# RWKV scan on one core: the last level of the chunk inverse is applied to the solution, one square and one sum share their weights, and half of the turned blocks are made by transposes

## The chip, the cores and the metric

The kernel runs on one core of one Trainium2 chip. The metric is the device time of one execution, in microseconds (us). The kernel computes a two-layer block and a final mixture of experts; the change touches one stage of it, the scan of the second layer's RWKV mixer.

## The reference

Only the scan matters here. For each of 16 heads of width 64, and for two directions (forward over the tokens, and reversed), a 64x64 state is carried over 256 context tokens and then 512 latent tokens:

```python
def step(s, inp):
    rt, wt, kt, vt, at, bt = inp
    sa = jnp.einsum('bhij,bhj->bhi', s, at)
    s = s * wt[:, :, None, :] + sa[..., None] * bt[:, :, None, :] + vt[..., None] * kt[:, :, None, :]
    y = jnp.einsum('bhij,bhj->bhi', s, rt) if with_out else None
    return s, y
```

The output y is wanted for the latent tokens only. All is float32.

## The kernel before, in words

**Chunks.** The scan goes by chunks of 64 tokens. Inside a chunk the rule "each token's correction depends on those of the tokens before it" is a triangular system of 64 unknowns, so a chunk needs the inverse X of a triangular 64x64 matrix. The inverse does not depend on the state and is made ahead. Then the state streams through the chunks: a right-hand side `rh` from state and values, the solution `uu` = X times the right-hand side, then the output `out` and the next state `zz`.

**Units.** A unit n (0 to 23) is one pair of heads (m = n // 3) and one third of the tokens (256), in both directions. It has 4 chunks per direction, and two heads side by side on the partitions 0 to 63 and 64 to 127 (`halves`). Every small product is therefore 64 rows by 64 columns, and is issued twice, once for each head: `blocks` multiplies four chunks, `turned` transposes blocks by a product with the identity, `gram` makes the products of the operands. One `yield` stands behind each pair of such products. Groups called crossed put a head's result on the other head's partitions, straight ones leave it where it is, so a crossed pair and a straight pair use the four quarters of the array between them.

**The inverse.** `gram` gives P and the masked 16-wide diagonal blocks N (`NP` holds N and its transpose). X = I + N, then three squarings (`squares 0` to `squares 2`) with three sums (`X add` 0 to 2) invert the 16-wide blocks. Two levels follow (16 to 32, 32 to 64). Each makes P·X (`PX`), masks it (`M`), and adds a product with the turned X (`X turned`, copied to `XT`): `XM` 1 and `XM` 2. Between them `XMT` brings the turned X up to date as well.

**The stream.** In each unit and chunk position `sub` (0 to 3): PE `rh` (L2585, L2591), ACT copies it (L2955), PE `uu` (L2605), ACT copies it (L2960), PE `out` (L2621, L2625, L2629) and `zz` (L2647, L2650, L2654), DVE scales the new state (L2845), and the next `rh` needs that.

**Order.** The order of the work on each engine is written down in tables (`CROSSED_AT`, `STRAIGHT_AT`, `WHOLE_AT`, `ACT_AT`, `DVE_AT`, `POOL_AT`). A step of unit n stands at 12n + its number; each engine issues its steps in the order of these numbers and waits only for semaphores. On PE, `together` merges three sorted lists (crossed, straight, whole-array products), a pair of products taking 0.06 on this scale. PSUM has 8 banks, taken in turn, and a product's bank is taken when its group is issued.

**Lines.** L2557 is `blocks` (both squares, sums, PX, XM, XMT), L2567 is `turned` (X turned, bk, v turned), L2548 is `gram` (gram, ka, br). L2823, L2829, L2833, L2835 and L2839 are DVE's sums and masks of the inverse, L2983 is ACT's copy of squares 0 and 1, L2987 of squares 2, L2992 of the turned X.

Of the kernel before, what the change touches and what calls it, by code (L numbers as in the profile page):

```python
# [548 lines left out]
def plan_layer1(K, w_at):  # L549
# [28 lines left out]
    r.NP = K.flat(1024).rearrange("p (d x g c) -> p d x g c", d=2, x=2, g=4)  # L578
    r.Pf, r.Arb = ([K.alloc(2, 4, 64) for _ in range(2)] for _ in range(2))
# [17 lines left out]
    r.X = [K.alloc(2, 4, 64) for _ in range(3)]  # L597
# [1819 lines left out]
def stream_at(part, first, gap=3):  # L2417
# [8 lines left out]
WHOLE_AT = {"lora": 0, "norms": -4.07, "y centred": 45.15, "y var": 50.54, "coef": 55.93, "gates": 58.5}  # L2426
ACT_AT = {"lora": 0.08, "e2": 5.86, "aa": 9.31, "gram": 12.54, "squares 0": 13.58, "squares 1": 16.34, "squares 2": 18.4,
          "X turned": 21.73, "bk": 23.26, **stream_at("rh", 31.43), **stream_at("uu", 32.71), **stream_at("out", 34.01),
          "kk sq": -20.77, "kk rstd": 0.94, "v turned": 2.81, "gate parts": 43.96, "y centred": 45.54, "y rstd": 51.73,
          "coef rows": 41.29}  # L2430
DVE_AT = {"B": 2, "B mid": 4.84, "B before": 7.26, "aa": 10.96, "bb": 10.19, "gram": 12.44, "X": 13.22, ("X add", 0): 15.85,
          ("X add", 1): 18.22, ("X add", 2): 20.51, ("M", 1): 22.97, ("XM", 1): 25.99, "ka": 24.09, ("M", 2): 27.36,
          "Arb": 26.03, ("XM", 2): 28.86, "kk sum": -4.02, "kk": 6.18, "gate rest": 45.52, "y scaled": 52.84, "rw y": 57.78,
          **stream_at("zz", 33.7)}
POOL_AT = {"gain": 4.56, "kr": -0.33, "bb": 0.21, "rr": 6.97, "k dir": -2.48}
# [24 lines left out]
class Unit:  # L2460


    def __init__(self, K, d, n):
        r = K.rw
        self.d, self.n, self.m, self.b = d, n, n // 3, n % 3
        self.s = r.dirs[d]
        self.key = (d, n)
        self.items = PAIRS[d][self.b]
        self.lo = min(self.items) * 128
        self.hi = self.lo + 256  # L2470
        self.lat = self.b > 0
# [6 lines left out]
        self.NP, self.M, self.Pf = r.NP[:, d], r.M[:, d], r.Pf[n % 2][:, d]  # L2478
# [60 lines left out]
def rw_pe(K):  # L2539
# [57 lines left out]
    def solution(n, sub):  # L2597

        pe.wait_ge(K.at("rh in", n, sub), K.at("X", n, 5))
        bank = K.bank("uu", n, sub)  # L2600
        for u in both(K, n):
            g = u.chunk(sub)[0]
            ps = bank[:, 64 * u.d:64 * u.d + 64]
            for hd, o in halves():
                mm = pe.e.matmul(ps[half(1 - hd)], u.X[o, g, :], r.RH[o, u.d, :], start=True, stop=True)  # L2605
            if u.d:
                mm.then_inc(*pe.up(("uu", n, sub)))
            yield
# [26 lines left out]
    def states(n, sub):  # L2635
# [4 lines left out]
        pe.wait_ge(K.at("BK", n))  # L2640
        for u in both(K, n):
            g, cs, x = u.chunk(sub)
            first = u.b == 0 and sub == 0
            ps = bank[:, 64 * u.d:64 * u.d + 64]
            if not first:
                for hd, o in halves():
                    pe.e.matmul(ps[o], K.ident[o, o], r.zm[sub % 2][o, u.d, :], start=True, stop=False, skip_group_check=True)  # L2647
                yield
            for hd, o in halves():
                pe.e.matmul(ps[o], u.BK[o, 1, g, :], r.V[u.m % 2][o, x, :], start=first, stop=False, skip_group_check=True)  # L2650
# [9 lines left out]
    def products(step, n):  # L2660
# [7 lines left out]
        if step in ("squares 0", "squares 1"):  # L2668
            lev = int(step[-1])
            pe.wait_ge(K.at("NP", n, lev))  # L2670
            for u in both(K, n):
                ps = K.bank(("squares", lev), *u.key)
                yield from blocks(ps, 0, u.NP[:, 1], u.NP[:, 0], 0)
                yield from blocks(ps, 256, u.NP[:, 0], u.NP[:, 1], 0, (("squares", lev), *u.key))
# [21 lines left out]
        if step[0] == "XM":  # L2696
            pe.wait_ge(K.at("M", n, step[1]), K.at("XT", n, step[1]))
# [32 lines left out]
        if step[0] == "uu":  # L2730
            yield from solution(n, step[1])
        if step[0] == "out":
# [61 lines left out]
def rw_dve(K):  # L2794
# [8 lines left out]
    for at, step, n in rw_order(DVE_AT):  # L2803
# [17 lines left out]
        if step[0] == "X add":  # L2821
            v.wait_ge(v.now(), K.at(step, n))
            v.e.tensor_tensor(four(X), four(X), K.ps.of(step, n), ADD).then_inc(*v.up(("X", n, step[1] + 1), free(step, n)))  # L2823
        if step[0] == "M":
            px = "PX", step[1]
            v.wait_ge(K.at(px, n), K.at("XMT", n) if step[1] == 2 else {})
            if n and step[1] == 1:
                v.wait_ge(K.at(("XM", 2), n - 1))
            v.e.tensor_tensor(r.M, p4(K.ps.of(px, n)), per_direction(r.masks[step[1]]), MUL).then_inc(  # L2829
                *v.up(("M", n, step[1]), free(px, n)))  # L2830
        if step == ("XM", 1):
            v.wait_ge(v.now(), K.at(("XM", 1), n), K.at("XMT", n))
            v.e.tensor_tensor(four(X), four(X), K.ps.of(step, n), ADD).then_inc(*v.up(("X", n, 4), free(step, n)))  # L2833
            v.wait_ge(K.at("XT", n, 1))
            v.e.tensor_tensor(four(r.XT), four(r.XT), K.ps.of("XMT", n), ADD).then_inc(  # L2835
                *v.up(("XT", n, 2), free("XMT", n)))
# [110 lines left out]
def rw_act(K):  # L2947
    a, s, r = K.a1, K.act, K.rw
    s.wait_ge(K.at("half bias"))
    for at, step, n in rw_order(ACT_AT):  # L2950
        m = n // 3
        if step[0] == "rh":
            sub = step[1]
            s.wait_ge(K.at("rh", n, sub), K.at("uu", *previous(n, sub)) if n or sub else {})
            s.e.activation(r.RH.rearrange("p d c -> p (d c)"), K.ps.of("rh", n, sub)[:, 0:128], ACT.Copy).then_inc(  # L2955
                *s.up(("rh in", n, sub), free("rh", n, sub)))
        if step[0] == "uu":
# [20 lines left out]
        if step in ("squares 0", "squares 1"):  # L2978
            lev = int(step[-1])
            s.wait_ge(K.at("X", n, 0), K.at(("X add", 0), n) if lev else {})  # L2980
            for u in both(K, n):
                s.wait_ge(K.at(("squares", lev), *u.key))
                s.e.activation(u.NP.rearrange("p x g c -> p (x g c)"), K.ps.of(("squares", lev), *u.key), ACT.Copy).then_inc(  # L2983
                    *s.up(("NP", n, lev + 1), free(("squares", lev), *u.key)))
# [5 lines left out]
        if step == "X turned":  # L2990
            s.wait_ge(K.at("X turned", n), K.at(("XM", 2), n - 1) if n else {})
            s.e.activation(four(r.XT), K.ps.of("X turned", n), ACT.Copy).then_inc(*s.up(("XT", n, 1), free("X turned", n)))  # L2992
# [1389 lines left out]
```

## Time and profile before

| | |
|---|---|
| median of 3 runs | 3533.31 us (3530.44 to 3544.45) |
| the profiled execution's own time | 3544.86 us |
| its span | 3543.0 us |
| the scan's stretch | 1508 to 2160 us from the span's start |
| matmul instructions in that stretch | 21268 |
| PE busy in that stretch | 546.72 of 652.00 us |
| DVE busy | 415.21 us |
| ACT busy | 349.64 us |

The span is what the profiler saw between the first and last instruction; the profiled execution is 1.86 us longer. Busy is the union of the records of an engine; a matmul's record runs from its start to its modelled end, so small matmuls overlap and a busy PE is not one that streams all the time. A float32 product appears as two LDWEIGHTS records and two MATMUL records.

### The profile page before, as it was taken

What the parts mean: (1) busy time and instruction counts of PE and PEld (TensorE: products, weight loads), DVE (VectorE), ACT (ScalarE), POOL (GpSimd) and SP (SyncE); (2) the same over time, 40 slices, a digit from 0 to 9 for tenths busy, and PEclk for the clock granted to TensorE, in tenths of its full rate; (3) what the DMA queues carried; (4) which work ended last, traced back from release to release, by engine and by line L of the source; (5) the groups of instructions that cost most, each with busy time, mean ns of one, the idle gap of its engine ahead of it and who ended that gap; (6) DMA issues with size and microseconds to landing.
All of it is one profiled execution on the core that took longest, in us unless ns stands there. A gap on an engine that the chain in (4) does not pass through costs nothing. (4 is left out here: it accounts for less than half of the span.)

```text
span 3543.0 us, 84567 instructions
## 1 busy us (share of the span) xinstructions
PE 3212.4 (91%) x38814; PEld 2573.9 (73%) x38814; DVE 1534.2 (43%) x2633; ACT 1148.9 (32%) x2233; POOL 404.1 (11%) x512
## 2 busy tenths in 40 slices
PE   7998998999999889888888889999989997999998
PEld 5766976799999848777777776899977775534343
DVE  3354446433233363266666663434435554111112
ACT  3343233322122332355555553322343333000001
POOL 0000013100000210133323320000012101000000
PEclk8999999999999999999999999999999998799999
DMA  4394144111111211000000002222121124499996
GB/s 186 115 363 163 48 184 167 72 72 72 48 72 67 73 48 48 8 6 6 6 13 30 7 4 97 95 96 96 72 70 48 66 92 172 198 428 410 412 424 285
DMA packets 35284, 437.81 MB, mean 124 GB/s; under 512 B 5040, under 2 KB 5648, under 8 KB 9200
## 3 DMA queue, kind: packets, MB, share of 16 engines
q1 hardware_dynamic: 29856, 414.10, 29.5%
q0 software_dynamic: 5072, 18.30, 1.6%
q8 instruction: 305, 5.00, 0.6%
q14 instruction: 51, 0.42, 0.0%
HBM read 425.56 MB, written 6.82 MB: 122 GB/s over the span
## 5 line engine op out<-in xcount | busy, mean ns | idle before, releaser
L755 PE MATMUL ps<-part 128*128 128x512 f32 (+1 forms) x4656 | 857.2, 346 | 41.8 <-DVE part L998 15.5
L755 PEld LDWEIGHTS ps<-part 128*128 128x128 f32 x4656 | 734.6, 194 | 160.6 <-issue 18.5
L2057 PE MATMUL ps<-part 128*128 128x256 f32 x1856 | 515.9, 278 | 3.3 <-DVE part L2098 3.3
L2058 PE MATMUL ps<-part 128*128 128x256 f32 x1856 | 515.7, 278 | 0.0
L2059 PE MATMUL ps<-part 128*128 128x256 f32 x1856 | 515.7, 278 | 0.0
L4012 PE MATMUL ps<-part 128*64 128x512 f32 x1536 | 374.9, 608 | 28.8 <-DMA part<-in_wg 14.1
L2098 DVE TENSOR_TENSOR part<-part 128x1024 fp32r<-128x1024 f32 x128 | 158.1, 1235 | 488.3 <-ACT part L2087 488.3
L2557 PE MATMUL ps<-part 64*64 64x64 f32 x9984 | 308.6, 222 | 57.2 <-issue 45.0
L2057 PEld LDWEIGHTS ps<-part 128*128 128x128 f32 x1856 | 348.8, 188 | 4.0 <-ACT part L2161 3.8
L2058 PEld LDWEIGHTS ps<-part 128*128 128x128 f32 x1856 | 350.9, 189 | 0.2
L2059 PEld LDWEIGHTS ps<-part 128*128 128x128 f32 x1856 | 348.4, 188 | 0.0
L2557 PEld LDWEIGHTS ps<-part 64*64 64x64 f32 x9984 | 280.6, 136 | 71.7 <-issue 54.2
L4012 PEld LDWEIGHTS ps<-part 128*64 128x64 f32 x1536 | 125.9, 140 | 258.2 <-issue 188.7
L2087 ACT ACTIVATE part<-part 128x1024 fp32r<-128x1024 f32 x128 | 135.9, 1061 | 480.1 <-PE ps L2076 316.7
L730 DVE TENSOR_TENSOR part<-part 128x2048 fp32r<-128x2048 f32 x53 | 121.3, 2293 | 236.5 <-ACT part L725 219.8
L2074 PE MATMUL ps<-part 128*128 128x256 f32 (+1 forms) x608 | 183.0, 301 | 14.8 <-DVE part L2121 11.4
L2075 PE MATMUL ps<-part 128*128 128x256 f32 (+1 forms) x608 | 182.3, 300 | 0.0
L2076 PE MATMUL ps<-part 128*128 128x256 f32 (+1 forms) x608 | 182.2, 300 | 0.0
L845 POOL TENSOR_TENSOR part<-part 128x512 f32<-128x512 f32 (+1 forms) x42 | 49.2, 1181 | 1155.0 <-ACT part L837 1154.5
L2074 PEld LDWEIGHTS ps<-part 128*128 128x128 f32 x608 | 115.3, 190 | 21.7 <-DVE part L2121 12.6
L4089 DVE TENSOR_TENSOR part<-part,ps 128x512 f32<-128x512 f32 x32 | 22.0, 688 | 246.8 <-PE ps L3986 118.4
L725 ACT ACTIVATE part<-part 128x2048 fp32r<-128x2048 f32 x54 | 102.9, 1910 | 61.0 <-PE ps L755 54.6
(429 smaller groups left out, 5021.0 us busy)
## 6 DMA issues: line engine op xcount, KB each, us to landing
part<-in_ada_w SPq DMA_DIRECT2D x36, 2048.0 KB, 9.1
part<-in_mlp_w SPq DMA_DIRECT2D x32, 2048.0 KB, 7.8
part<-in_wg SPq DMA_DIRECT2D x32, 2048.0 KB, 14.6
part<-in_wu SPq DMA_DIRECT2D x32, 2048.0 KB, 13.1
part<-in_wd SPq DMA_DIRECT2D x32, 2048.0 KB, 13.9
part<-in_b_in SPq DMA_DIRECT2D x8, 2048.0 KB, 7.7
part<-in_ab_w_in SPq DMA_DIRECT2D x7, 2048.0 KB, 7.9
part<-in_rkv SPq DMA_DIRECT2D x6, 2048.0 KB, 7.6
```

Source lines behind the costliest of these rows:

```text
L730: v.e.tensor_tensor(self.rest(g), self.tile(g), self.first(g), SUB).then_inc(*v.up((name, "split", g)))
L755: mm = pe.e.matmul(ps[:, j * n:j * n + n], lhs, rhs, start=k == ks[0] and i == 0, stop=k == ks[-1] and i == 2)
L2057: pe.e.matmul(ps, wh[:, k, :], hi[:, k, x], start=k == 0, stop=False)
L2058: pe.e.matmul(ps, wh[:, k, :], lo[:, k, x], start=False, stop=False)
L2059: mm = pe.e.matmul(ps, wl[:, k, :], hi[:, k, x], start=False, stop=k == 7)
L2074: pe.e.matmul(ps, wh[:, k, :], hi[:, k, x0:x1], start=k == 0, stop=False)
L2075: pe.e.matmul(ps, wh[:, k, :], lo[:, k, x0:x1], start=False, stop=False)
L2076: mm = pe.e.matmul(ps, wl[:, k, :], hi[:, k, x0:x1], start=False, stop=k == 7)
L2087: s.e.activation(b.W[t % 2][0], src, ACT.Copy).then_inc(*s.up(self.key("rounded", t), self.key("split", t), *([("free", "w") + self.key("w ...
L2098: v.e.tensor_tensor(wl, src, wh, SUB).then_inc(*v.up(self.key("split", t), *([("free", "w") + self.key("w", p)] if c == 3 else [])))
L2557: mm = pe.e.matmul(ps[half(hd ^ flip), o + g * 64:o + g * 64 + 64], lhs[h, g, :], rhs[h, g, :], start=True, stop=True)
L4012: mm = pe.e.matmul(ps[half(p), :], lhs(k, p), K.panel(8, 512, w, g, c, p)[:, k, :], start=k == 0, stop=k == 7)
```

## The change

It does five things in the scan.

1. `XM` 2 and `XMT` are gone. The last level is not put into X; instead the stream multiplies twice. With X4 the inverse after the first level, T = X4 · RH (step `t`), then UU = T + M2 · T (step `mt`, the sum by DVE). `uu` and its copy become `t` and its copy.
2. `squares 1` takes the block `NP[:, 1]` as weights once, and streams the square's operand and X behind it in one product of 128 columns. `X add` 0 as a product is gone; its sum is read out of the same bank.
3. The turned half of the second squaring goes to a bank of its own (`squares turned`).
4. In `turned`, the product of a block with the identity becomes a transpose where the result lies on partitions 0 to 63.
5. M2, Pf, X and T get other places, M2 has two buffers, and every table is new.

```diff
-            for hd, h in halves():
-                mm = pe.e.matmul(ps[half(hd ^ flip), o + i * 64:o + i * 64 + 64], block[h, :], K.ident[h, h], start=True,
-                                 stop=True)
+                out = ps[half(hd ^ flip), o + i * 64:o + i * 64 + 64]
+                if hd ^ flip:
+                    mm = pe.e.matmul(out, block[h, :], K.ident[h, h], start=True, stop=True)
+                else:
+                    mm = pe.e.transpose(out, block[h, :], K.ident[h, h])
...
+    def last_level(n, sub):
+
+        pe.wait_ge(K.at("t in", n, sub), K.at("M", n, 2))
+        bank = K.bank("mt", n, sub)
+        for u in both(K, n):
+            g = u.chunk(sub)[0]
+            for hd, o in halves():
+                mm = pe.e.matmul(bank[o, 64 * u.d:64 * u.d + 64], u.M2[o, g, :], r.T[o, u.d, :], start=True, stop=True)
+            if u.d:
+                mm.then_inc(*pe.up(("mt", n, sub)))
+            yield
...
+        if step == "squares 1":
+            pe.wait_ge(K.at("NP", n, 1), K.at("X", n, 0))
+            for u in both(K, n):
+                ps = K.bank(("squares", 1), *u.key)
+                for g in range(4):
+                    i, j = 8 * u.d + g, 16 + 8 * (n % 3) + 4 * u.d + g
+                    for hd, h in halves():
+                        mm = pe.e.matmul(ps[h, 128 * g:128 * g + 128], u.NP[h, 1, g, :], r.NX[h, i:j + 1:j - i, :],
+                                         start=True, stop=True)
+                    if g == 3:
+                        mm.then_inc(*pe.up((("squares", 1), *u.key)))
+                    yield
+            ps = K.bank("squares turned", n)
+            for u in both(K, n):
+                yield from blocks(ps, 256 * u.d, u.NP[:, 0], u.NP[:, 1], 0, *([("squares turned", n)] if u.d else []))
...
-        if step == "XMT":
-            ps = K.bank("XMT", n)
-            pe.wait_ge(K.at("M", n, 1), K.at("XT", n, 1))
-            for u in both(K, n):
-                yield from blocks(ps, 256 * u.d, u.M, u.XT, 0, *([("XMT", n)] if u.d else []))
...
+        if step == ("X add", 0):
+            for u in both(K, n):
+                sums = K.ps.of(("squares", 1), *u.key).rearrange("p (g x c) -> p g x c", g=4, x=2)
+                v.wait_ge(v.now(), K.at("NP from", *u.key))
+                v.e.tensor_tensor(u.X, u.X, sums[:, :, 1, :], ADD).then_inc(
+                    *v.up(("X", n, 1), free(("squares", 1), *u.key)))
...
-        if step == ("XM", 2):
-            v.wait_ge(v.now(), K.at(step, n))
-            v.e.tensor_tensor(four(X), four(X), K.ps.of(step, n), ADD).then_inc(*v.up(("X", n, 5), free(step, n)))
+        if step[0] == "mt":
+            sub = step[1]
+            v.wait_ge(K.at("t in", n, sub), K.at("mt", n, sub), K.at("streamed", *previous(n, sub, 2)) if 4 * n + sub >= 2 else {})
+            v.e.tensor_tensor(r.UU[sub % 2].rearrange("p d c -> p (d c)"), r.T.rearrange("p d c -> p (d c)"),
+                              K.ps.of("mt", n, sub)[:, 0:128], ADD).then_inc(*v.up(("uu in", n, sub), free("mt", n, sub)))
...
-            s.wait_ge(K.at("uu", n, sub), K.at("streamed", *previous(n, sub, 2)) if 4 * n + sub >= 2 else {})
-            s.e.activation(r.UU[sub % 2].rearrange("p d c -> p (d c)"), K.ps.of("uu", n, sub)[:, 0:128],
-                           ACT.Copy).then_inc(*s.up(("uu in", n, sub), free("uu", n, sub)))
+            s.wait_ge(K.at("t", n, sub), K.at("uu in", *previous(n, sub)) if n or sub else {})
+            s.e.activation(r.T.rearrange("p d c -> p (d c)"), K.ps.of("t", n, sub)[:, 0:128], ACT.Copy).then_inc(
+                *s.up(("t in", n, sub), free("t", n, sub)))
```

ACT's part of `squares 1` becomes, per direction, a copy of the 64-wide halves of the shared bank (256 columns), and one copy of `squares turned` (512 columns); it waits for `squares turned` first. The PE tables before and after:

```diff
-CROSSED_AT = {"gram": 12.06, "X turned": 22.53, ("PX", 1): 23.08, ("XM", 1): 25.44, ("PX", 2): 27.45, ("XM", 2): 29.2,
-              **stream_at("rh", 31.91), **stream_at("uu", 32.91), **stream_at("out", 34.11)}
-STRAIGHT_AT = {"squares 0": 13.61, ("X add", 0): 15.5, "squares 1": 16.4, ("X add", 1): 17.77, "squares 2": 19.06,
-               ("X add", 2): 20.57, "bk": 22.59, "ka": 23.84, "XMT": 24.39, "br": 26.58, **stream_at("zz", 34.08),
-               "v turned": 2.27}
+CROSSED_AT = {"gram": 12.04, "X turned": 22.4, ("PX", 1): 23.46, ("XM", 1): 26.9, ("PX", 2): 29.81, **stream_at("rh", 29.55),
+              **stream_at("out", 30.8), **stream_at("t", 30.02)}
+STRAIGHT_AT = {"squares 0": 14.67, "squares 1": 17.81, ("X add", 1): 18.86, "squares 2": 20.41, ("X add", 2): 20.92,
+               "bk": 21.97, "ka": 23.84, "br": 29.32, **stream_at("zz", 30.8), "v turned": -3.56, **stream_at("mt", 30.39)}
```

## Rows read from the trace of the kernel before

**Rows 1.** The page: busy time of three engines, and the instruction queue.

```profile
PE 3212.4 (91%) x38814; PEld 2573.9 (73%) x38814; DVE 1534.2 (43%) x2633; ACT 1148.9 (32%) x2233; POOL 404.1 (11%) x512
...
q8 instruction: 305, 5.00, 0.6%
```

**Rows 2.** Windows, the scan: length, busy and (records) of PE, PEld, DVE, ACT, POOL; PEclk, DMA.

```profile
1508.00:2160.00 652.00, 546.72 (x21268) 470.05 (x21266) 415.21 (x833) 349.64 (x921) 187.79 (x307) 0.99 0.04 10
```

**Rows 3.** DMA queues over the scan, 1508 to 2160: packets, MB, share.

```profile
q8 instruction: 166, 2.72, 1.8%
```

**Rows 4.** Windows of PE alone, cut at six stops that follow one another.

```profile
1584.40:1587.50 3.10, 2.56 (x128) 1.00 0.02 5
1587.50:1591.10 3.60, 2.94 (x128) 1.00 0.02 7
1591.10:1594.70 3.60, 3.02 (x121) 1.00 0.02 5
1594.70:1598.10 3.40, 2.61 (x135) 1.00 0.02 5
1598.10:1601.90 3.80, 3.31 (x127) 1.00 0.02 4
1601.90:1605.80 3.90, 2.42 (x127) 1.00 0.01 4
```

**Rows 5.** DMA queues over those six turns, 1584.4 to 1605.8.

```profile
q8 instruction: 6, 0.10, 1.8%
```

**Rows 6.** Timeline of PE around one stop: start, length, what, idle before.

```profile
1597.04 0.34 PE L2557 MATMUL ps<-part 64*64 64x64 f32 x5
1598.16 0.27 PE L2557 MATMUL ps<-part 64*64 64x64 f32 x1 [0.79 <-issue]
```

**Rows 7.** Waits of PE in the scan: total us, times, longest.

```profile
PE ps L2557 <- issue: 45.0, 55, 1.6
PE ps L2548 <- issue: 7.0, 9, 1.3
...
PE ps L2557 <- ACT part L2983: 6.0, 21, 0.7
...
PE ps L2591 <- DVE part L2845: 3.6, 10, 0.4
...
PE ps L2650 <- issue: 0.3, 1, 0.3
```

**Rows 8.** Groups of PE in the scan, by form: busy, mean ns, idle before.

```profile
L2557 PE MATMUL ps<-part 64*64 64x64 f32 x9984 | 308.6, 222 | 57.2 <-issue 45.0 <-ACT part L2983 6.0 <-ACT part L2968 1.5
```

**Rows 9.** Timeline, right-hand side copied, solution, its copy: PE and ACT.

```profile
1803.06 0.27 ACT L2955 ACTIVATE part<-ps 128x128 f32<-128x128 f32 x1
...
1803.40 0.27 PE L2605 MATMUL ps<-part 64*64 64x64 f32 x2
...
1803.51 0.22 PE L2605 MATMUL ps<-part 64*64 64x64 f32 x1
...
1803.57 0.22 PE L2605 MATMUL ps<-part 64*64 64x64 f32 x1
...
1803.63 0.22 PE L2605 MATMUL ps<-part 64*64 64x64 f32 x1
...
1803.98 0.28 ACT L2960 ACTIVATE part<-ps 128x128 f32<-128x128 f32 x1 [0.65 <-PE ps L2605]
```

**Rows 10.** Groups of DVE and ACT in the scan, the operations that the change touches.

```profile
L2983 ACT ACTIVATE part<-ps 128x512 f32<-128x512 f32 x96 | 56.4, 596 | 61.5 <-PE ps L2557 59.3 <-PE ps L2605 1.9
...
L2823 DVE TENSOR_TENSOR part<-part,ps 128x512 f32<-128x512 f32 x72 | 49.5, 687 | 35.6 <-PE ps L2557 34.3
...
L2845 DVE TENSOR_TENSOR part<-ps,part 128x128 f32<-128x128 f32 x85 | 24.7, 290 | 43.6 <-PE ps L2654 33.7 <-PE ps L2629 8.3
...
L2977 ACT ACTIVATE part<-ps 128x256 f32<-128x256 f32 x48 | 17.2, 375 | 10.3 <-DVE part L2810 9.6
```

**Rows 11.** Source line L3839, the router's 32 transposes: count, ns min/median/max, forms.

```profile
L3839 PEld LDWEIGHTS ps<-part x32: 138/141/146, 2996.1 to 3001.2; 128*128 128x128 f32 x32
L3839 PE MATMUL ps<-part x32: 272/273/328, 2996.1 to 3001.3; 128*128 128x128 f32 x32
```

More of the change, by code:

```diff
@@ L596, in plan_layer1 @@
     r.ops = [K.alloc(2, 4, 256) for _ in range(3)]
-    r.X = [K.alloc(2, 4, 64) for _ in range(3)]
+    r.Pf = [K.alloc(2, 4, 64) for _ in range(2)]
+    r.M2 = [K.alloc(2, 4, 64), K.sc.rearrange("p (d g) j c -> p d g (j c)", d=2)]
+    r.T = K.shaped(K.Cf[:, 1600:1728], 2, 64)
     r.RH, r.UU, r.zm = K.alloc(2, 64), [K.alloc(2, 64) for _ in range(2)], [K.alloc(2, 64) for _ in range(2)]
@@ L2426 @@
[L2426 to L2430, printed above, removed]
@@ new lines @@
+STRAIGHT_AT = {"squares 0": 14.67, "squares 1": 17.81, ("X add", 1): 18.86, "squares 2": 20.41, ("X add", 2): 20.92,
+               "bk": 21.97, "ka": 23.84, "br": 29.32, **stream_at("zz", 30.8), "v turned": -3.56, **stream_at("mt", 30.39)}
+WHOLE_AT = {"lora": 0, "norms": -5.23, "y centred": 50.47, "y var": 51.71, "coef": 56.9, "gates": 57.86}
+ACT_AT = {"lora": 0.62, "e2": 6.15, "aa": 7.96, "gram": 12.7, "squares 0": 16.09, "squares 1": 19.24, "squares 2": 20.84,
+          "X turned": 21.86, "bk": 23.39, **stream_at("rh", 29.27), **stream_at("out", 32.02), "kk sq": -11.23,
+          "kk rstd": -2.39, "v turned": -2.62, "gate parts": 28.85, "y centred": 50.55, "y rstd": 52.98, "coef rows": 38.82,
+          **stream_at("t", 30.46)}
@@ L2438, in happens @@
+DVE_AT = {"B": 3.6, "B mid": 5.64, "B before": 5.73, "aa": 9.75, "bb": 10.06, "gram": 13.77, "X": 14.7, ("X add", 0): 19.35,
+          ("X add", 1): 22, ("X add", 2): 22.7, ("M", 1): 24.82, ("XM", 1): 29.35, "ka": 25.18, ("M", 2): 30.61,
+          "Arb": 30.39, "kk sum": -2.24, "kk": 0.85, "gate rest": 47.43, "y scaled": 56.6, "rw y": 58.84,
+          **stream_at("zz", 32.37), **stream_at("mt", 31.34)}
+POOL_AT = {"gain": 15.54, "kr": 6.67, "bb": 15.53, "rr": 15.55, "k dir": 6.3}
 def happens(step, n):
@@ L2597, in solution @@
     def solution(n, sub):
-        pe.wait_ge(K.at("rh in", n, sub), K.at("X", n, 5))
-        bank = K.bank("uu", n, sub)
+        pe.wait_ge(K.at("rh in", n, sub), K.at("X", n, 4))
+        bank = K.bank("t", n, sub)
         for u in both(K, n):
             g = u.chunk(sub)[0]
-            ps = bank[:, 64 * u.d:64 * u.d + 64]
             for hd, o in halves():
-                mm = pe.e.matmul(ps[half(1 - hd)], u.X[o, g, :], r.RH[o, u.d, :], start=True, stop=True)
+                mm = pe.e.matmul(bank[half(1 - hd), 64 * u.d:64 * u.d + 64], u.X[o, g, :], r.RH[o, u.d, :], start=True,
+                                 stop=True)
             if u.d:
-                mm.then_inc(*pe.up(("uu", n, sub)))
+                mm.then_inc(*pe.up(("t", n, sub)))
+            yield
[8 more added lines that the diff above has]
+                mm.then_inc(*pe.up(("mt", n, sub)))
             yield
@@ L2640, in states @@
         pe.wait_ge(K.at("BK", n))
+        first = n % 3 == 0 and sub == 0
         for u in both(K, n):
             g, cs, x = u.chunk(sub)
-            first = u.b == 0 and sub == 0
             ps = bank[:, 64 * u.d:64 * u.d + 64]
-            if not first:
-                for hd, o in halves():
+            for hd, o in halves():
+                if not first:
                     pe.e.matmul(ps[o], K.ident[o, o], r.zm[sub % 2][o, u.d, :], start=True, stop=False, skip_group_check=True)
-                yield
-            for hd, o in halves():
                 pe.e.matmul(ps[o], u.BK[o, 1, g, :], r.V[u.m % 2][o, x, :], start=first, stop=False, skip_group_check=True)
@@ L2977, in rw_act @@
                 s.e.activation(u.Pf, src[:, :, 1, :], ACT.Copy).then_inc(*s.up(("Pf", *u.key), free("gram", *u.key)))
-        if step in ("squares 0", "squares 1"):
-            lev = int(step[-1])
-            s.wait_ge(K.at("X", n, 0), K.at(("X add", 0), n) if lev else {})
+        if step == "squares 0":
+            s.wait_ge(K.at("X", n, 0))
             for u in both(K, n):
-                s.wait_ge(K.at(("squares", lev), *u.key))
-                s.e.activation(u.NP.rearrange("p x g c -> p (x g c)"), K.ps.of(("squares", lev), *u.key), ACT.Copy).then_inc(
-                    *s.up(("NP", n, lev + 1), free(("squares", lev), *u.key)))
+                s.wait_ge(K.at(("squares", 0), *u.key))
+                s.e.activation(u.NP.rearrange("p x g c -> p (x g c)"), K.ps.of(("squares", 0), *u.key), ACT.Copy).then_inc(
+                    *s.up(("NP", n, 1), free(("squares", 0), *u.key)))
+        if step == "squares 1":
+            s.wait_ge(K.at("squares turned", n))
+            for u in both(K, n):
+                s.wait_ge(K.at(("squares", 1), *u.key))
+                s.e.activation(u.NP[:, 0], K.ps.of(("squares", 1), *u.key).rearrange("p (g x c) -> p g x c", g=4, x=2)[
+                    :, :, 0, :], ACT.Copy).then_inc(*s.up(("NP", n, 2), ("NP from", *u.key)))
+            s.e.activation(r.NP[:, :, 1].rearrange("p d g c -> p d (g c)"),
+                           K.ps.of("squares turned", n).rearrange("p (d c) -> p d c", d=2), ACT.Copy).then_inc(
+                *s.up(("NP", n, 2), free("squares turned", n)))
         if step == "squares 2":
@@ L2990, in rw_act @@
         if step == "X turned":
-            s.wait_ge(K.at("X turned", n), K.at(("XM", 2), n - 1) if n else {})
-            s.e.activation(four(r.XT), K.ps.of("X turned", n), ACT.Copy).then_inc(*s.up(("XT", n, 1), free("X turned", n)))
+            s.wait_ge(K.at("X turned", n), K.at(("XM", 1), n - 1) if n else {})
+            s.e.activation(four(r.XT), K.ps.of("X turned", n), ACT.Copy).then_inc(*s.up(("XT", n), free("X turned", n)))
         if step == "bk":
```

52 lines of the change are left out of this document (25 added, 27 removed).

## The prediction

> **What bounds the kernel now.** I read the page first: PE is busy 91% of the span [rows 1]. Then the windows over the scan, the only stage that the change touches: 652 us, PE busy 547, DVE 415, ACT 350 [rows 2]. So PE's order decides, and DVE and ACT have room. The reader's next question should be what PE does in the 105 us when it is idle. The waits answer it in an unusual way: on L2557 alone 45.0 us in 55 stops stand as "issue", no semaphore named, while the longest named waits are 6.0 us (ACT's copy of the squares) and 3.6 us (the new state) [rows 7]. Over all lines of PE the twelve "issue" entries of that view (the largest 45.0, the smallest 0.3) add up to 83.5 us in 102 stops, against some 18 us with a name.
>
> The timeline shows one such stop: `blocks` in the middle of a group, five matmuls at 1597.04, then nothing until 1598.16 [rows 6]. What comes in during these stops? The DMA view has one queue that carries instructions: 166 packets in the scan [rows 3]. The scan has 21268 matmul and 21266 weight-load records [rows 2], together 42534, so one packet for 256.2 of them; the whole page gives the same (77628 records, 305 packets, 254.5) [rows 1]. And when windows are cut at six stops that follow one another, each holds 121 to 135 matmuls, 128 on the mean, which is 256 instructions with their weight loads [rows 4], and the six hold six packets [rows 5]. PE stops when it has used up 256 instructions and the next packet is not there. These six turns took 21.4 us, 3.57 each. That is my floor for a turn; the mean over the scan is 652 / 166 = 3.93 us.
>
> So the scan is, for most of its time, bound by how many instructions PE is given, not by what they stream. How much work lies in a turn without the stop? The idle of a stop is counted from the modelled end of a record (222 ns), though the next product may start 58 ns behind (four starts of L2605 between 1803.40 and 1803.63 [rows 9], records of 222 ns [rows 8]); so each stop is 0.16 us longer than its entry, and the 102 stops cost 83.5 + 16 = 100 us. Work without them: 552 us, 3.33 a turn.
>
> **What the change does, part by part.** Counted per unit, in products (each is two weight loads and two matmuls, four instructions, as L2557 has 9984 matmul records for 24 units of 208 products [rows 8]):
>
> - `XM` 2 and `XMT` gone: 16 products each, minus 32.
> - `squares 1` with shared weights: before, 32 products and 16 of `X add` 0; after, 16 of 128 columns and 16 turned. Minus 16.
> - Stream: `uu` becomes `t`, 16 and 16; `mt` is new, plus 16.
> - Sum: minus 32 products, minus 128 instructions.
> - `turned`: X turned 16, bk 32, v 8 products, half of them transposes, 28. The router's 32 transposes left 32 matmul and 32 weight-load records [rows 11], so a transpose is two instructions where the product is four: minus 56.
>
> Together 184 fewer of some 1,800 a unit, 4416 in 24 units, 4416 / 256.2 = 17.2 packets: 166 becomes 148.8 in the scan, 305 becomes 288 on the page.
>
> What PE streams hardly falls. Straight columns: `squares 1` and its sum move the same 48 blocks of 64 columns, `XMT` (16) is made up by `mt` (16); crossed ones lose 16. A turned pair still lasts as long as its product half. So on streaming alone nothing would be won; I take it as equal, 552 us.
>
> New waits. A stream hop costs PE: from ACT's start to the next product 0.34 us (1803.06 to 1803.40), from the last product to ACT's start 0.35 (1803.63 to 1803.98) [rows 9], 0.6 to 0.7 for ACT; DVE's 0.29 operation [rows 10] is priced alike. What hides it is what the tables put between. With a pair at 0.117 us (two starts of 58 ns) I counted this filler in both tables. Before: `uu` stands well ahead of `zz` and `out`, and the shortages are `X add` 1 (0.4 each unit), `X add` 0 and `rh` 0 (0.6 to 0.7 in one unit of three), smaller ones, 1.3 us a unit. After: behind `mt` only one pair or two of `zz` (0.23 us) come before the product that needs UU, in three of four positions, a shortage of 0.3 each; `t` to `mt` 0.2 once; `X add` 2 comes right behind `X add` 1 in one unit of three (0.85); 1.8 in all. Plus 0.5 x 24 = 12 us: work 564 us.
>
> DVE and ACT: DVE loses three 512-column operations (0.69 each [rows 10]) and gains two of 256 columns (unseen as such; between 0.29 and 0.69) and four of 0.29, so between 0.3 us less and 0.5 us more a unit; ACT's copies of `squares 1` go from 2 x 0.60 to 2 x 0.38 + 0.60 [rows 10]. Both lie behind PE, at 415 and 350 of 652 us [rows 2]; if that cover went, 0.5 us a unit would be 12 us. PSUM: per unit `mt` takes four banks more and three groups fewer than before take one, one more is `squares turned`; a ring that turns faster is not priced, from 0 to those same 12 us.
>
> **The sum.** 564 / 148.8 = 3.79 us of work a turn, 0.46 more than 3.33. If the fetch went on setting every turn, a turn would stay at 3.93: 148.8 x 3.93 = 585 us, 67 us won. If every turn passed its longer work on: 4.39 x 148.8 = 653 us, nothing won. Now 102 of 166 turns end in a stop, so 4 in 10 pass added work on; as work nears the floor more do, say 6 in 10. I take half: 3.93 + 0.23 = 4.16, x 148.8 = 619.6 us, 32 us less. The profiled execution took 3544.86, so 3513 by that one; the median of the runs is 11.6 lower, and on it the forecast is 3501 us.
>
> **A rule against it.** No transpose in the trace of before runs in a 64-column tile: those of L3839 are 128 by 128 [rows 11]. The Trainium skill, TensorEngine Tiling (Array Packing), Restrictions and Gotchas, lists column tiling and transpose mode for float32 inputs as mutually exclusive. By that rule the new transposes would be none in fact; by the router's rows they halve the instructions. It gives a rival, next.
>
> **The rivals.**
>
> - *Transposes give nothing.* Each issues four instructions after all: 56 x 24 = 1344 back, 5.2 packets, 154.0 turns with 3.66 of work, 3.93 + 0.17 = 4.10, 631 us: 21 won, 3512. For it: no row of a 64-wide transpose. Against: two instructions each in every transpose seen. Chance 0.10.
> - *The whole gain.* The new waits fall into the fetch stops and a turn stays at 3.93: 67 won, 3466. For it: stops are long (up to 1.6 us [rows 7]). Against: 4 in 10 turns have none. Chance 0.10.
> - *No change.* Each packet gained is used up by its longer work, 0 to 15 us won, 3518 to 3533. For it: streamed columns are the same. Chance 0.15.
> - *Slower: the stream's longer loop.* One more PE, DVE and back hop in each of 96 positions. Were `t` to `mt` and `mt` to `zz` both uncovered, 1.2 x 96 = 115 us, 103 above those counted: work 667 us, 4.48 a turn, above the floor, and some stops left (0.1 a turn): 682 us, 30 slower, 3563. It decides from work of 640 us on, 0.8 us a position. For it: the loop has a hop more, and PE issues in order. Against: named waits are only 18 us of 652 now, and a stop for a packet covers a hop. Chance 0.10.
>
> My forecast itself, 15 to 50 won (3483 to 3518), has 0.55.
>
> **How the numbers follow.** What this kernel's measurement can tell from no change is 0.5%, 17.7 us. Faster by more: the whole gain 0.10, nine tenths of the forecast 0.50, six tenths of the first rival 0.06: 0.66, with a little of the third 0.68. Slower: 0.10 and a tail, 0.11. The same: 0.21. The range goes from the whole gain, 3466, to the no-change case, 3533.
>
> **What would show it.** Right: some 288 packets in the instruction queue of the page, some 149 in the scan; about 19,100 matmul records in the scan; stops still 256 instructions apart but fewer and shorter; a mean turn between 4.0 and 4.3 us; PE's waits for ACT's `t` copy, DVE's `mt` sum and `X add` 1 newly among the named ones, together under 40 us. L2567's successor shows 64-wide transposes with one record each. Wrong: a turn still at 3.93 (the gain is then double), or named waits on `mt` of 80 us and more (the loop). The prediction would also be wrong at its root if stops did not move with the instruction count, which would mean that the packets only go along with them.

## The result, and the profile after

The changed kernel takes 3740.61 us (median of 4 runs, 3737.3 to 3747.84) against 3531.88 us before: a ratio of 1.0597, 95% interval 1.058 to 1.0614. It is 209 us slower, where 3501 us was forecast.

The page of the changed kernel, busy time and the instruction queue, beside [rows 1]:

```profile
PE 3461.5 (92%) x36606; PEld 2730.4 (73%) x36606; DVE 1548.4 (41%) x2705; ACT 1161.1 (31%) x2268; POOL 401.0 (11%) x512
...
q8 instruction: 288, 4.72, 0.5%
```

2208 matmuls fewer and 288 instruction packets for 305: these terms came out to the unit. And yet PE is busy 249 us longer. The windows over the scan, columns as in [rows 2]:

```profile
1508.00:2348.00 840.00, 784.63 (x18460) 617.41 (x18458) 413.40 (x869) 353.46 (x929) 177.79 (x294) 0.84 0.03 7
```

Fewer matmuls (18460 for 21268) fill more time (785 us for 547), and the mean granted clock is 0.84 where it was 0.99. The first whole-array product of the scan and the last output product stand at 1489.7 and 2170.5 us before, at 1477.5 and 2374.9 after: the scan went from 681 to 897 us, 216 us more, where the two profiled executions differ by 203 us of span, so the whole loss is in it. Windows of PE (length, busy, matmuls, clock), cut where the clock changes:

```profile
1752.30:1772.50 20.20, 20.18 (x226) 0.50 0.01 2
1772.70:1796.40 23.70, 22.82 (x685) 1.00 0.01 3
1796.60:1806.70 10.10, 10.10 (x121) 0.50 0.01 2
1806.90:1830.60 23.70, 20.29 (x731) 1.00 0.02 5
```

In 30 of 78 us the clock is at its lower level of 1.2 GHz, and PE issues 11 matmuls per us there, 30 at 2.4 GHz. The same stretches for the transposes alone (L2575):

```profile
1752.30:1772.50 20.20, 5.62 (x26) 0.50 0.01 2
1772.70:1796.40 23.70, 1.25 (x6) 1.00 0.01 3
1796.60:1806.70 10.10, 3.15 (x19) 0.50 0.01 2
1806.90:1830.60 23.70, 1.39 (x6) 1.00 0.02 5
```

The transposes sit in the slow stretches, and the last six of a fast one just ahead of the fall. The timeline of PE shows what they do, first at full clock, ahead of the fall at 1796.6:

```profile
1794.21 0.24 PE L2575 MATMUL ps<-part 64*64 64x64 f32 x1
1794.38 0.33 PE L2573 MATMUL ps<-part 64*64 64x64 f32 x2
1794.63 0.24 PE L2575 MATMUL ps<-part 64*64 64x64 f32 x1
1794.81 0.32 PE L2573 MATMUL ps<-part 64*64 64x64 f32 x2
```

One transpose, then the product of the other head (L2573, two matmuls), then the next transpose: 0.42 us from pair to pair, where the prediction had 0.117 us, two starts, for a pair of products. From the last start of one kind to the first of the other the trace has 0.15 us (to a transpose) and 0.17 us (back), the median over all changes at full clock; from one start to the next among products it is 0.03 us on the mean. At the lower clock, with both lanes in a turned group:

```profile
1800.19 0.32 PE L2575 MATMUL ps<-part 64*64 64x64 f32 x2
1800.43 0.48 PE L2573 MATMUL ps<-part 64*64 64x64 f32 x4
1800.84 0.32 PE L2575 MATMUL ps<-part 64*64 64x64 f32 x2
1801.09 0.48 PE L2573 MATMUL ps<-part 64*64 64x64 f32 x4
```

0.65 us from round to round, with 0.24 us at each change. Nothing of the other kind starts until what runs is nearly over: in the median of all 480 changes each way, 0.07 us before the modelled end of the last record. So the two kinds hardly overlap, and PE's pipeline runs nearly empty at each change. The source view of L2575:

```profile
L2575 PEld LDWEIGHTS ps<-part x672: 104/126/128, 1471.5 to 2348.3; 64*64 64x64 f32 x168
L2575 PE MATMUL ps<-part x672: 241/310/313, 1471.5 to 2348.3; 64*64 64x64 f32 x168
```

672 transposes with one matmul record each: they are true transposes, of two instructions. The changes of kind, counted from the starts of all PE records, are 480 there and as many back, half of them at the lower clock (237 of those to a transpose).

### The profile page after: what moved, and what is told of

It reads as the page before. It is cut to its first block and busy times, and to the rows that moved or that the text cites. A ratio compares the mean times of both kernels' runs of the same rounds, so it can differ in the third digit from the quotient of the medians.

```text
span 3746.1 us, 80369 instructions
## 1 busy us (share of the span) xinstructions
PE 3461.5 (92%) x36606; PEld 2730.4 (73%) x36606; DVE 1548.4 (41%) x2705; ACT 1161.1 (31%) x2268; POOL 401.0 (11%) x512
## 3 DMA queue, kind: packets, MB, share of 16 engines
q8 instruction: 288, 4.72, 0.5%
## 5 line engine op out<-in xcount | busy, mean ns | idle before, releaser
L760 PEld LDWEIGHTS ps<-part 128*128 128x128 f32 x4656 | 733.1, 194 | 162.0 <-issue 18.4
L2062 PEld LDWEIGHTS ps<-part 128*128 128x128 f32 x1856 | 348.4, 188 | 4.0 <-ACT part L2166 3.8
L2064 PEld LDWEIGHTS ps<-part 128*128 128x128 f32 x1856 | 348.9, 188 | 0.0
L2063 PEld LDWEIGHTS ps<-part 128*128 128x128 f32 x1856 | 348.4, 188 | 0.2
L2561 PE MATMUL ps<-part 64*64 64x64 f32 x6912 | 251.8, 236 | 24.3 <-issue 7.4
L2561 PEld LDWEIGHTS ps<-part 64*64 64x64 f32 x6912 | 231.1, 149 | 35.0 <-issue 15.4
L2079 PE MATMUL ps<-part 128*128 128x256 f32 (+1 forms) x608 | 181.3, 298 | 14.8 <-DVE part L2126 11.4
L2573 PE MATMUL ps<-part 64*64 64x64 f32 x1344 | 194.8, 304 | 0.0
L2573 PEld LDWEIGHTS ps<-part 64*64 64x64 f32 x1344 | 115.7, 175 | 44.4
L2575 PE MATMUL ps<-part 64*64 64x64 f32 x672 | 133.9, 286 | 0.0
```

Source lines behind the costliest of these rows:

```text
L760: mm = pe.e.matmul(ps[:, j * n:j * n + n], lhs, rhs, start=k == ks[0] and i == 0, stop=k == ks[-1] and i == 2)
L2062: pe.e.matmul(ps, wh[:, k, :], hi[:, k, x], start=k == 0, stop=False)
L2063: pe.e.matmul(ps, wh[:, k, :], lo[:, k, x], start=False, stop=False)
L2064: mm = pe.e.matmul(ps, wl[:, k, :], hi[:, k, x], start=False, stop=k == 7)
L2079: pe.e.matmul(ps, wh[:, k, :], hi[:, k, x0:x1], start=k == 0, stop=False)
L2561: mm = pe.e.matmul(ps[half(hd ^ flip), o + g * 64:o + g * 64 + 64], lhs[h, g, :], rhs[h, g, :], start=True, stop=True)
```

## The experiments

Each was compared with the kernel before on the same chip; ratios are against it. "Slower than e1" is the difference of two ratios, times 3532 us; from the intervals of the two, such a difference is uncertain by some 10 to 13 us. Cuts of code are shortened, and the tables of DVE and ACT are left out of them unless said.

**e1_no_transposes**

```diff
-                if hd ^ flip:
-                    mm = pe.e.matmul(out, block[h, :], K.ident[h, h], start=True, stop=True)
-                else:
-                    mm = pe.e.transpose(out, block[h, :], K.ident[h, h])
+                mm = pe.e.matmul(out, block[h, :], K.ident[h, h], start=True, stop=True)
```

> The changed kernel with the turned blocks made by products again, all else as changed. Theory A (each change between a transpose and a product makes PE drain, and the sparser PE then falls to the lower clock; the rest of the change gains as forecast): 293 instruction packets on the page, scan at clock 0.97 or more, total 3495 to 3530, near 3511. Theory B (the stream's longer loop and the new order are what costs; the transposes are a minor part): total above 3600, clock still below 0.9 in the scan.

Measured: 3533.66 us, ratio 1.0034 (1.0011 to 1.0058), 293 packets. Theory A's first half holds: 0.056 of the 0.060 is gone with the transposes. Its second half does not: the rest gains nothing and loses 12 us. Windows over the scan, and the largest waits of PE:

```profile
1508.00:2160.00 652.00, 571.26 (x19852) 489.94 (x19850) 424.15 (x904) 366.66 (x967) 189.36 (x308) 0.98 0.03 10
```

```profile
PE ps L2668 <- DVE part L2870: 9.6, 47, 0.5
PE ps L2561 <- issue: 9.6, 15, 1.5
PE ps L2561 <- ACT part L3027: 6.9, 10, 0.7
PE ps L2552 <- issue: 6.6, 9, 1.3
PE ps L2621 <- DVE part L2862: 5.6, 12, 0.9
PE ps L2561 <- DVE part L2850: 4.5, 16, 0.4
PE ps L2621 <- ACT part L3020: 3.5, 5, 0.8
```

L2668 is `zz`'s product with UU, waiting for the sum behind `mt` (L2870); L2621 is `mt`, waiting for the mask M2 (L2862) and for ACT, busy with its copy of squares 1 (L3020); L2561 waits for the copy of `squares turned` (L3027) and for sums of X. Over all lines, "issue" fell from 83.5 us in 102 stops to 27.0 us in 40, and the waits with a name rose from 18.2 us in 50 to 50.3 us in 130. PE is also busy 24.5 us more for 1416 matmuls fewer in the same window: over the whole scan of each, "issue" fell by 56 us, named waits rose by 36 and busy by 21, so the two scans are equally long.

**e2_only_transposes**: the kernel before with `turned` as changed, nothing else.

```diff
-                mm = pe.e.matmul(ps[half(hd ^ flip), o + i * 64:o + i * 64 + 64], block[h, :], K.ident[h, h], start=True,
-                                 stop=True)
+                out = ps[half(hd ^ flip), o + i * 64:o + i * 64 + 64]
+                if hd ^ flip:
+                    mm = pe.e.matmul(out, block[h, :], K.ident[h, h], start=True, stop=True)
+                else:
+                    mm = pe.e.transpose(out, block[h, :], K.ident[h, h])
```

> The kernel before with half of the turned blocks made by transposes, nothing else. Theory A: 3700 to 3780, with switch rounds of 0.3 us or more each and a clock near 0.83 in the scan. Theory B: below 3600.

Measured: 3699.52 us, 1.0512 (1.0484 to 1.0539), 180 us slower; the clock over 1508 to 2160 us is 0.87. The transposes alone make nearly all of the loss; theory B falls.

**e3_grouped_transposes**

```diff
+        for hd, h in halves():
+            if not hd ^ flip:
+                for i, block in enumerate(blocks_of):
+                    pe.e.transpose(ps[half(0), o + i * 64:o + i * 64 + 64], block[h, :], K.ident[h, h])
+        yield
+        for i, block in enumerate(blocks_of):
+            h = half(1 ^ flip)
+            mm = pe.e.matmul(ps[half(1), o + i * 64:o + i * 64 + 64], block[h, :], K.ident[h, h], start=True, stop=True)
```

> The changed kernel, but each turned group issues its 4 (or 8) transposes in a row and its products behind them, so that the changes between the two kinds fall from some 480 to about 160. Theory A: the loss shrinks with the number of changes, to some 3570 (3540 to 3620), and the clock recovers most. Theory B, or a cost that goes with the transposes themselves and not with the changes: above 3690.

Measured: 3565.74 us, 1.0126 (1.0098 to 1.0155). The same 672 transposes, 112 changes there and back instead of 480, and 32 us over e1 instead of 199. Its scan runs at full clock:

```profile
1508.00:2160.00 652.00, 595.93 (x18554) 504.52 (x18550) 419.37 (x883) 358.74 (x945) 184.64 (x304) 1.00 0.03 10
```

So it is the change of kind that costs, and the clock falls with the alternation of the two kinds, not with the number of transposes; why it does is not shown. Transposes in runs are still slower than products (e1), though they save 5 packets.

**e7_few_transposes** and **e8_x_transposes**: e1 with transposes in one use alone.

```diff
-                if hd ^ flip:
+                if hd ^ flip or not (done and done[0][0] == "v turned"):
```

```diff
-                if hd ^ flip:
+                if hd ^ flip or not (flip):
```

> As e1, with transposes in v turned alone: 96 of the 672. Theory A (a change to a transpose and back costs 0.2 us of drain at full clock; the low clock comes only when many follow on one another): 15 to 25 us slower than e1, clock in the scan 0.96 or more. Rival (transposes themselves pull the clock down): 50 us or more.

> As e1, with transposes in X turned alone (192 of the 672, all in one lane and at one place of a unit). Theory A, drain alone: 192 x 0.2 = 38 us slower than e1 (30 to 50), clock above 0.93. Above 80 us, with a clock under 0.9, would say that even one group a unit lowers the clock.

Measured: e7 3573.72 us, 1.0106 (1.008 to 1.0133), 25 us over e1 for 96 transposes, clock 0.97 in the scan; e8 3584.07 us, 1.0145 (1.0117 to 1.0173), 39 us over e1 for 192, clock 0.98. That is 0.26 and 0.20 us for a transpose that stands between products. In e8 the clock is hardly touched: 45 us of its scan are at the lower level, 43 in e1. In e7 it is not left alone, with 63 us, and 23 of its 96 transposes run at the lower level; its 0.26 us holds some of that.

**e4_unshared_weights**: e1 with the shared product as two.

```diff
-                        mm = pe.e.matmul(ps[h, 128 * g:128 * g + 128], u.NP[h, 1, g, :], r.NX[h, i:j + 1:j - i, :],
-                                         start=True, stop=True)
+                        for x in (i, j):
+                            o = 128 * g + 64 * (x == j)
+                            mm = pe.e.matmul(ps[h, o:o + 64], u.NP[h, 1, g, :], r.NX[h, x, :], start=True, stop=True)
```

> As e1, but the product of 128 columns in the second squaring is issued as two of 64 with the same weights loaded twice, into the same bank and in the same order: the same columns streamed, 64 instructions more per unit, 6 packets more. Theory F (PE's instruction packets set the pace): 12 to 24 us slower than e1, 299 packets. Rival G (what is streamed and waited for sets the pace, packets only go along): within 5 us of e1.

Measured: 3539.85 us, 1.0049 (1.003 to 1.0068), 299 packets: 5 us over e1, with intervals that overlap. That is about 1 us a packet and nearer to the rival than to theory F, but the difference is too uncertain to exclude the 12 us at which theory F begins. The two profiled scans, 682.1 and 680.9 us, differ by 1.2 us.

**e11_halved_products**: the same question asked of the kernel before. (Its result is not the reference's, and the runs do not show why; its time and what it issues are read.)

```diff
-                    mm = pe.e.matmul(out[half(hd ^ flip), 2 * it + j], lhs[o, t], rhs[o, :, t], start=True, stop=True)
+                    for x in range(out.shape[2]):
+                        mm = pe.e.matmul(out[half(hd ^ flip), 2 * it + j, x:x + 1], lhs[o, t], rhs[o, x:x + 1, t],
+                                         start=True, stop=True)
```

and each whole-array product but `gates` in two halves of its columns.

> The kernel before with each product of 128 columns or more in the scan issued in two halves of its columns: the same columns streamed in the same order, no wait more, some 70 instructions more per unit, 6 to 7 packets on the page (311 or 312). Theory F: in the kernel before, where 6 turns in 10 end in a stop for a packet, each packet more costs 2 to 3.9 us: 13 to 25 us slower than before. Rival G: within 5 us.

Measured: 3559.5 us, 1.0065 (1.0045 to 1.0085), 23 us slower for 6 packets more (311). The DMA view and the windows of its scan, 1508 to 2160:

```profile
q8 instruction: 166, 2.72, 1.8%
```

```profile
1508.00:2160.00 652.00, 541.83 (x21272) 494.47 (x21270) 396.85 (x813) 345.14 (x903) 185.68 (x306) 0.99 0.04 10
```

166 packets and 21272 matmuls in 652 us, as in [rows 2, 3], though its instructions are smaller: the pace is one of instructions. Six packets at 3.93 us are 23.6 us, and 23 were lost (16 to 30 by the interval). Windows of PE over the whole scan (first whole-array product to last output product), of before and of e11:

```profile
1489.70:2170.70 681.00, 561.89 (x21626) 0.98 0.04 10
1488.60:2196.20 707.60, 584.91 (x22428) 0.98 0.04 10
```

The scan of e11 is 27 us longer, but PE's busy time grew by 23 of them, the "issue" stops by 9 (83.4 us in 102 to 92.4 in 107), and the named waits fell by 6. If only the arrival of packets set the pace, smaller instructions should have left PE busy no longer and made the stops longer. A rival is therefore left: each instruction costs PE time of its own. Some 1,630 more of them in 23 us are 14 ns each, and a product of four instructions starts every 58 ns [rows 9], 14.5 ns each. e11 shows that instructions count, not that it is by packets alone.

**e12_loop_without_hop**: e1 with `out` and `zz` reading T.

```diff
-            pe.wait_ge(K.at("uu in", n, sub))
+            pe.wait_ge(K.at("t in", n, sub))
...
-            s.wait_ge(K.at("t", n, sub), K.at("uu in", *previous(n, sub)) if n or sub else {})
+            s.wait_ge(K.at("t", n, sub), *([K.at("uu in", *previous(n, sub)), K.at("streamed", *previous(n, sub))] if n or sub else []))
```

> As e1 (no transposes), but out and zz read T in place of UU: mt and DVE's sum are issued as before, and nothing waits for them in the stream (the last level is so left out of the result). The same instructions, 293 packets. Theory L (the hop behind mt, uncovered at 12.3 us of PE waits in e1, and the wait for M2 are what ate the packets' gain): 8 to 20 us faster than e1, which would be 3514 to 3526 on a base of 3534 and level with before or below. Rival (the waits are covered elsewhere or only move): within 5 us of e1.

Measured: 3525.99 us, 0.9984 (0.9966 to 1.0003): level with before and 18 us faster than e1, with the same instructions. Windows of PE over the whole scan, e1 and e12:

```profile
1486.70:2167.60 680.90, 583.02 (x20044) 0.97 0.03 10
1477.70:2148.60 670.90, 563.90 (x20044) 0.98 0.04 10
```

Of the 20 us between the two profiled executions (3542.2 and 3522.1 us of span), 10 are in the scan. Most of these lie in its first and last two units: between the first products of units 2 and 22, a unit takes 26.78 us in e1 and 26.68 in e12. The other 9 or so lie ahead of the scan, in work that is the same. So the time agrees with theory L, but of the difference between the profiled executions at most half can be the hop. Nor is the hop wholly gone, since the copy of T still waits for the last sum. The rest of the gain is not there either: its named waits still add up to 50.8 us, others having grown. One thing more is to be read here: for the same instructions PE is busy 19 us less. So "busy" moves with the waits and the clock (43 us of e1's scan are at the lower level, 24 of e12's), and part of the 21 us that e1 has above before need not be work.

**e5_more_room**: e1 with room behind `mt` and `X add` 1.

```diff
-CROSSED_AT ... **stream_at("out", 30.8), **stream_at("t", 30.02)}
+CROSSED_AT ... **stream_at("out", 31.2), **stream_at("t", 30.02)}
-STRAIGHT_AT ... ("X add", 2): 20.92, ... **stream_at("zz", 30.8) ...
+STRAIGHT_AT ... ("X add", 2): 21.45, ... **stream_at("zz", 31.2) ...
```

> As e1 (no transposes), with three numbers of the PE tables moved so that more lies between dependent steps: zz and out 0.4 later (behind mt), X add 2 0.53 later (behind X add 1). No instruction more or less. Theory W (what e1 lost again are the new uncovered waits behind mt and X add 1): 8 to 20 us faster than e1, 3514 to 3526 on the base of 3534. Rival (these waits lie in the stops for instruction packets anyway): within 4 us of e1.

Measured: 3578.08 us, 1.0134 (1.011 to 1.0159), 35 us slower than e1: both theories miss. Waits of PE in its scan:

```profile
PE ps L2561 <- DVE part L2850: 16.0, 11, 1.5
...
PE ps L2775 <- ACT part L3038: 11.7, 14, 0.9
PE ps L2621 <- ACT part L2992: 10.4, 22, 0.7
```

The wait of `zz` for the sum behind `mt` fell from 9.6 to 2.7 us, but `mt` (L2621) now waits for the copy of T (L2992, 10.4 us), `lora` (L2775) for the copy of BK (L3038, 11.7 us), and the blocks for the first sum of X (L2850) 16.0 us where e1 had 4.5. Steps moved on PE alone, with ACT's and DVE's order left, opened waits elsewhere in this run.

**e6_only_shared_weights** and **e9_shared_moved**: the kernel before with the shared weights alone. The first cut is e6 against before, the second e9 against e6. DVE's `X add` 0 moves too (15.85 to 17.2 in e6, 17.0 in e9), and in e9 ACT's `squares 2` (18.4 to 19.1) and DVE's `X add` 1 (18.22 to 19.3).

```diff
-STRAIGHT_AT = {"squares 0": 13.61, ("X add", 0): 15.5, "squares 1": 16.4, ("X add", 1): 17.77, "squares 2": 19.06,
+STRAIGHT_AT = {"squares 0": 13.61, "squares 1": 16.0, ("X add", 1): 17.77, "squares 2": 19.06,
```

```diff
-STRAIGHT_AT = {"squares 0": 13.61, "squares 1": 16.0, ("X add", 1): 17.77, "squares 2": 19.06,
+STRAIGHT_AT = {"squares 0": 13.61, "squares 1": 15.5, "squares 2": 17.77, ("X add", 1): 18.9,
```

> The kernel before with the shared weights of the second squaring alone (16 products and 64 instructions fewer per unit, 6 packets), squares 1 and X add 0 moved a little in the tables, no other table changed. Theory F (packets set the pace): 299 packets, 10 to 20 us faster than before. Rival G (streamed columns and waits set it): within 5 us of before, or slower by the one copy more.

> As e6 (the kernel before with the shared weights alone), with squares 2 now ahead of X add 1 on all engines and squares 1 earlier, since in e6 PE waited 43.9 us for DVE's sum of X, 22 times up to 2.4 us. Theory C (the shared product puts two ACT copies and two DVE sums in a row ahead of X add 1, and what stands in between decides): the wait on that sum falls under 15 us and the total to within 15 us of before. Theory F would add: below before, by 5 to 20 us. Rival (any move in these tables costs some 50 us, whatever it is): 3570 or more on the base of 3532.

Measured: e6 3586.91 us, 1.015 (1.0129 to 1.0172); e9 3565.16 us, 1.0084 (1.0066 to 1.0102). In e6 PE waits for DVE's sum of X (L2842):

```profile
PE ps L2560 <- DVE part L2842: 43.9, 22, 2.4
```

This sum now stands behind the turned squares, two ACT copies and a sum for the other direction. With the order changed in e9 the wait is spread, not gone:

```profile
PE ps L2560 <- DVE part L2846: 18.4, 14, 2.0
PE ps L2608 <- DVE part L2842: 17.2, 14, 1.2
PE ps L2560 <- DVE part L2842: 11.4, 9, 1.5
```

Theory C has the place right and was too hopeful of the cure. Sharing the weights saves 6 packets and makes the sum of X late, by 2.0 us a time in e6 (43.9 us in 22 waits); with tables moved by hand it lost 53 us (e6) and 30 us (e9), and in the new tables (e1 against e10, below) no gain is measured.

**e10_last_level_alone**: e1 with the second squaring and `X add` 0 as before.

```diff
-"squares 0": 14.67, "squares 1": 17.81,
+"squares 0": 14.67, ("X add", 0): 17.33, "squares 1": 17.81,
```

DVE's `X add` 0 moves from 19.35 to 18.3.

> As e1 (no transposes) with the second squaring and X add 0 done as before, X add 0 put back between squares 0 and squares 1: of the change, the last level on the solution and the tables are left. 299 packets. If the shared weights are what gains in e1 and the longer loop what loses: 5 to 15 us slower than e1. If the loop costs nothing and the late sum of X is what loses: 5 to 20 us faster than e1, below before.

Measured: 3545.04 us, 1.0034 (1.0015 to 1.0052), level with e1: neither of its two cases. Within some 10 us the shared weights do nothing in the new order, and the last level with its tables is the small loss. (The profiled scans would give the shared weights a little: 686.8 us here, 680.9 in e1.) With the tables goes one thing that the list of changes does not name and no run takes alone: in `zz` the product with the identity and the one with V now stand in one place of the order, where they had two.

No run that computes the reference beats the kernel before.

## Why the prediction was wrong, point by point

**The step that failed** is "A turned pair still lasts as long as its product half", and with it "I take it as equal, 552 us". A turned pair of a transpose and a product lasts 0.42 us at full clock, not 0.117, since the two kinds hardly overlap; I had priced the instruction, not its neighbours. The effect on the clock stood in no term at all. The rows could not have given the size, but they should have given the question: no transpose of before stood between products in another quarter of the array, so the cost had to be bounded from both sides, with a full latency of a matmul (0.22 us [rows 8]) at each change as a wide end. 672 transposes times twice 0.22 is 296 us, more than all I forecast to gain. My slower rival was a different mechanism (the stream's loop), priced at 30 us, and the range ended at 3533.

**How the 209 us are made up.** Ratio of after to e1: 199 us for the transposes. 480 changes there and back at the 0.20 us that e8 shows for each are 96 us; the remaining 100 us or so go with the clock, at its lower level for about a third of the scan (mean 0.84). The starts in the trace give much the same, as an estimate: from start to start, the gaps at changes of kind add up to 188 us. Of these, 31 us is what as many gaps among products take in e1 (0.033 us each), 120 us is what the changes add at full clock, and 37 us what the lower clock adds to them. The 2966 gaps among products at the lower clock take 0.064 us each instead of 0.034, which is 88 us more. Neither split is measured by itself; that the clock follows the alternation is shown by e3, where 672 transposes in 112 groups leave it at 1.00. The other 12 us are e1's.

**The rule of the Trainium skill** (TensorEngine Tiling (Array Packing), Restrictions and Gotchas) that column tiling and float32 transpose mode exclude each other was cited and turned into the wrong rival: that the transposes would issue as products. They issue two instructions each in 64-wide tiles, 672 of 672, so the trace does not bear the rule out as the rival had it. What the trace shows is that hardly anything else is active beside them; whether the rule means that, no run here shows. The same page, Tiling Modes, says that changing the tiling mode drains the engine; a gap of 0.15 to 0.17 us at full clock, as if PE drained, is what the changes of kind show here. That sentence speaks of tile shapes, not of transposes, and I did not carry it over.

**What was right.** The stops of the kernel before are stops for instructions: counted over its trace, all 102 lie at whole multiples of 256 instructions from one another, to within 8, and four in five of them end 1.25 to 1.53 us behind the landing of a packet. And instructions cost time: e11 adds six packets of them and loses 23 us with no column more, though it does not tell a packet's cost from an instruction's own. The counts, 184 instructions a unit and 288 packets, were exact (36606 matmul records for 38814, 2208 fewer, and as many weight loads fewer: 4416 instructions). For e1 the working gives turns of 4.10 us; from 1560 to 2100 us its trace has 133 packets, 4.06 us a turn (before 139, 3.88).

**What was mis-sized.** The new named waits were put at 12 us over 24 units. In e1 the named waits are 32 us more, the largest of them behind `mt` (9.6), of `mt` for M2 and for ACT (9.1), and for the sums and copies of the inverse (11.4). "I take it as equal, 552 us" misses in e1 as well, where no transpose is left: PE is busy 21 us longer over the scan with 1,580 matmuls fewer, and that is open but for what e12 says of it. And the 3.93 us turn of the whole scan includes its first and last units, which wait for other engines: in the middle, between the first products of units 2 and 22, the kernel before needs 27.15 us a unit and e1 26.78, a gain of 9 us in 24 units; the two scans are both 681 us from first to last product. The 21 us that the rival "transposes give nothing" had for this case did not come. That the two scans are equal while e1's timed runs are 12 us slower stays open: with e1's tables the start of the scan alone lies anywhere from 1477.4 (e8) to 1487.4 us (e7), and the profile of before is of other runs (median 3533.31 us) than those that e1 was compared with (3519.57). So the profiles can't settle 12 us.

**The chances.** 0.11 for slower was too little for an operation that no row showed in this setting.

## What to carry to other kernels

Price an instruction together with its neighbours: a transpose between small float32 products cost 0.15 and 0.17 us of PE here, before and behind it, and with many of them the clock. In runs of 4 or 8 they cost far less, but still more than products. When "issue" stands as the releaser of most of PE's idle time, divide the instruction packets into the time; if they come out at a constant turn, instructions are worth counting. But fewer of them need not be faster: in e1 twelve packets fewer took 56 us of stops away, and waits and busy time grew by as much. In a kernel whose order is written out for every engine, a step moved on one engine alone is likely to open waits on the others, as in e5.

## What the hardware showed that was not expected

- PE's instructions come in packets of 16 KB (4.72 MB in 288) for 256 instructions, and in the kernel before it stopped for them 102 times in the scan; six turns that ended so lasted 3.1 to 3.9 us [rows 4]. A 64-wide float32 product is four instructions, so a packet holds 64 of them.
- A change between a transpose and a product in 64 by 64 tiles, from start to start: 0.15 us to the transpose and 0.17 back at 2.4 GHz, 0.24 each way at 1.2 GHz.
- The granted clock fell to 1.2 GHz while transposes and products alternated (from 1794.21 on, the fall at 1796.6) and came back to 2.4 GHz in every unit; with the same transposes in runs (e3) the scan has 1.00 on the mean.
